# Two feed-forward layers in a one-core kernel: the first pair's down product as seven block products

## The chip, the cores and the metric

One core of a Trainium2 chip. The metric is the time of one execution in microseconds (us) of device time; below it is the median of 3 runs. In the profile PE is TensorE, DVE is VectorE, ACT is ScalarE, POOL is GpSimd, SP is SyncE, which issues most transfers.

## What is computed

One layer of a recurrent network on 1032 tokens (1024 of a prompt and 8 samples), width D = 1024, in float32. It begins and ends with a feed-forward layer of inner width 2816; between them lies a mixing stage, which the change leaves alone.

```python
def swiglu(x, w_gate, w_up, w_down):
    return (jax.nn.silu(x @ w_gate) * (x @ w_up)) @ w_down
...
    x = x + 0.5 * swiglu(rmsnorm(x, n1), f1g, f1u, f1d)
...
    x = x + m @ w_out
    x = x + 0.5 * swiglu(rmsnorm(x, n3), f2g, f2u, f2d)
```

## The kernel before

**Products.** A float32 operand is split into a high part (rounded, made by ACT) and a low part (the rest, made by DVE), and every product is three matmuls (`three`, L151): high x high, low x high, high x low. The halves of the input are 516 tokens each, and a matmul takes 258 tokens (columns) of one.

**Stages.** `ffn_tensor` (L585), `ffn_scalar`, `ffn_vector`, `ffn_gpsimd` and `ffn_sync` are the five engines' sides of one feed-forward layer. The layer is run twice, as `f1` and as `f2`. The inner width is 22 tiles, taken as 11 pairs. For the first pair, gate and up are eight plain products (`first_pair`, `plain`), each of 48 matmuls; the inputs are the four blocks B11, B21, B12, B22 (two row halves, two token halves). Every later pair i is a *group*: gate and up are seven products each (`product7`), by Strassen's scheme with the blocks B11, B21, B22 and four differences T1 to T4 of input blocks, and likewise seven weights (four of them sums of weight blocks, `unit_sums`). Each `product7` is 24 matmuls and leaves its result in a pair of PSUM banks; ACT copies some out (`snap`) and DVE adds others to them (`mix`), so that a later product may start on a pair only when the snap or mix of the one before is done.

**Down.** Group i (2 to 10) runs the down product of pair i-1 between its gate and its up (`down_pairs`): 7 blocks of hidden values, of which four are differences made by `hid_tees` on DVE, each split by ACT (`hid_high`) and DVE (`hid_low`); 168 matmuls. The parts that come out are added in DRAM to a running sum `x_sum` by accumulating transfers on POOL's queue (`ffn_gpsimd`). The down of the first pair is different: `down(True)`, a plain product of 24 output tiles of 344 tokens, 144 matmuls, right behind the first pair; DVE adds each tile to x (`add`), and then the updated x is copied to `x_sum` (8 transfers, L1260). Group 1 therefore has no down. The last pair's down is plain too, and is added to the x that has come back from `x_sum`.

**What sets the order.** Everything is written out by hand. Each engine works through its own list in order, and waits on counters of the others. Around the change these lists matter: on PE `first_pair`, `down(True)`, `group(1)`, then a loop over the groups; on ACT and DVE `first_pair`, `group_one` (and on DVE `behind_first` before it), then the loop. The T blocks of the input are made by DVE (`head_tees`), their high parts by ACT (`head_high`, L520), their low parts by DVE (`head_low`, L528); in the kernel before, T3, T1 and T4 are finished while PE runs `down(True)`. Weight slabs arrive in two buffers `raw` (`ffn_sync`). In the profile a weight's high part is L796 (L758 in the first pair), its low part L802 (L764), a weight sum L823, a snap L923, a mix L1082, a hidden product of the first pair L1045, an addition of `down` L1122, a hidden block's parts L858 and L865. DVE also does the model's small parameter arithmetic in group 1 of `f1` (`vector_between`, L3012 to L3028).

Of the kernel before, what the change touches and what calls it, by code (L numbers as in the profile page):

```python
# [32 lines left out]
NT = 3  # L33
# [25 lines left out]
FIRST_UNITS = 12  # L59
FIRST_SLABS = 6  # L60
FIRST_PRODUCTS = 8
LAST_DOWN = 3
DOWN_PAIRS = ((3, 2), (1, 0))
ADDED = 32 * (PAIRS - 1)
# [233 lines left out]
def units(i, n):  # L298

    return FIRST_UNITS + n if is_one(i) else i * 21 + (n + FIRST_UNITS + 14 - 42)  # L300


def prods(i, n):

    return FIRST_PRODUCTS + n if is_one(i) else i * 42 + (n + FIRST_PRODUCTS + 14 - 84)


def summed(i, n):

# [24 lines left out]

def prod_number(i, up, j):
    return (0, 7 if is_one(i) else 35)[up] + j + 1


def snap_number(i, up, n):
    return (0, 3 if is_one(i) else 19)[up] + n + 1  # L340


def mix_number(i, up, n):
    return (0, 3 if is_one(i) else 15)[up] + n + 1
# [16 lines left out]
def hid_count(i, j):  # L361
    return i * 7 + (32 - 7 + HID_ORDER.index(j) + 1)


def hid_tee(i, n):
    return i * 4 + (16 - 4 + n)
# [218 lines left out]
def ffn_tensor(pe, k, s):  # L585
    def plain(n, unit, pair, js, ready=None, between=None, parts=range(2), beside=None):

        for e in parts:
            pe.wait_ge(s.unit_lo, unit + e + 1)
            for g in range(2):  # L590
                if e == 1 and g == 1 and between:
                    between(pe)
                for kappa in range(KAPPAS):
                    if g == 0 and ready:
                        pe.wait_ge(s.norm.block_lo, block_count(js[e], kappa))
                    last = three(pe, k.bank[2 * pair + g][:, 0:QW], ffn_weight(s, (unit + e) % 6, kappa),
# [31 lines left out]
    def product7(i, up, j):  # L628

        pair = ((0, 2, 0, 1, 0, 1, 0), (2, 0, 2, 1, 2, 1, 2))[up][j]  # L630
        pe.wait_ge(s.unit_lo, units(i, unit_number(i, 2 * up, j)))
        if j in (T2, T3, T1, T4) and not up and is_one(i):
            pe.wait_ge(s.norm.block_lo, block_count(j, KAPPAS - 1))
        if j == 0:
            if not up:
                if is_one(i):
                    pe.wait_ge(s.down_used, KT * NT - 2)
                else:
                    pe.wait_ge(s.hidden, i * 4 - 3)
            elif is_one(i):  # L640
                pe.wait_ge(s.mixed, mixes(i, 1))
            else:
                pe.wait_ge(s.mixed, mixes(i, down_mix(1, 2, 1)))
        if j == 1:
            if not up:
                pe.wait_ge(s.hidden, i * 4)
            elif is_one(i):
                pe.wait_ge(s.silu, i * 4 + 4)
            else:
                pe.wait_ge(s.snap, snaps(i, down_snap(1, 3, 1)))  # L650
        if j == 2:
            pe.wait_ge(s.snap, snaps(i, snap_number(i, up, 0)))
        if j == 3 and up:
            if is_one(i):
                pe.wait_ge(s.mixed, mixes(i, 3))
        if j == 4:
            pe.wait_ge(s.snap, snaps(i, snap_number(i, up, 1)))
        if j == 5:
            pe.wait_ge(s.snap, snaps(i, snap_number(i, up, 2)))
        if j == 6:  # L660
            pe.wait_ge(s.mixed, mixes(i, mix_number(i, up, 1)))
# [7 lines left out]
    def down_pairs(i):  # L669

        for c in range(2):
            for j in range(7):
                if c == 0:
                    pe.wait_ge(s.unit_lo, units(i, unit_number(i, 1, j)))
# [11 lines left out]
    def four_ahead(i):  # L686

        pe.wait_ge(s.hidden_lo, s.hid_base + 5)
        pe.wait_ge(s.down_used, NT * KT)
        pe.wait_ge(s.mixed, mixes(i, mix_number(i, 1, 0)))  # L690
# [2815 lines left out]
```

## Time and profile before

| what | before |
|---|---|
| time, median of 3 runs | 2431.41 us (2430.89 to 2431.72) |
| span of the profiled execution (first to last instruction) | 2428.6 us |
| PE busy | 2415.6 us (99%), 19220 matmuls |
| DVE, ACT, POOL busy | 1739.7 us (72%), 1300.1 us (54%), 171.2 us (7%) |
| HBM traffic | 269.6 MB, 111 GB/s over the span |

The profile is one execution; its own time apart from its span is not given, so the median stands beside it, 2.8 us above the span. In a timeline row the first number is when the work began, the second how long it lasted; several equal instructions in a row are one line with their count. Successive instructions of one engine overlap a little: matmuls of 258 columns last 0.28 us each and start 0.12 us apart. In brackets stands how long the engine had been idle before, and what ended that. Idle time of an engine that holds nothing up costs nothing.

### The profile page before, as it was taken

The page shows a single profiled execution, that of the slowest core. Times are in us where ns is not written, and L with a number is a line of the kernel's source. Part 1 is how long each engine was busy: PE and PEld are TensorE (multiplying, and loading weights), DVE is VectorE, ACT ScalarE, POOL GpSimd, SP SyncE. Part 2 cuts the span into 40 slices and gives each one's busy share as a digit, 9 for nine tenths or more (in the row PEclk, how much of TensorE's full clock was granted, in tenths as well). Part 3 has the DMA queues.
Part 4 walks back from the last instruction along what each step waited for, and adds up shares of the span by engine and source line. Part 5 has one row for each costly group of instructions (what it writes and reads, how often), then busy time and mean ns, then how long its engine had stood idle before and what let it go on. Part 6 is the DMA issues. An engine that isn't in the chain of part 4 may idle for free.

```text
span 2428.6 us, 51528 instructions
## 1 busy us (share of the span) xinstructions
PE 2415.6 (99%) x19220; PEld 2400.9 (99%) x19220; DVE 1739.7 (72%) x2921; ACT 1300.1 (54%) x2206; POOL 171.2 (7%) x204
## 2 busy tenths in 40 slices
PE   9999999999999999999999999999999999999998
PEld 8999999999999999999999999999999999999998
DVE  8767767677689888887777775442676777777777
ACT  5355555555558676676666664211434555555554
POOL 0011111111120000000000000000200111111110
PEclk9999999999999999999999999999999999999999
DMA  4355555555541343333322235332023555555556
GB/s 144 106 123 121 121 121 121 122 121 121 135 182 54 95 114 81 88 97 100 109 90 87 69 138 178 140 131 87 18 103 88 123 122 122 122 122 122 122 123 197
DMA packets 137270, 278.34 MB, mean 115 GB/s; under 512 B 67024, under 2 KB 71632, under 8 KB 136656
## 3 DMA queue, kind: packets, MB, share of 16 engines
q1 hardware_dynamic: 114128, 192.39, 24.3%
q0 software_dynamic: 23040, 84.55, 18.4%
q8 instruction: 69, 1.13, 0.2%
q14 instruction: 33, 0.27, 0.0%
HBM read 154.80 MB, written 114.77 MB: 111 GB/s over the span
## 4 chain that ended last, share of the span: by engine, by line
PE 96%; DVE 2%; ACT 1%; DMA 1%; issue 0%; SPq 0%; DVEq 0%; ACTq 0%
PE banks L154 31%; PE banks L155 31%; PE banks L156 31%; PE banks L1819 1%; PE banks L1840 1%; PE banks L1850 1%; PE banks L1848 0%; PE banks L1854 0%; DMA x_sum<-f_snap 0%; DVE y L247 0%; DVE f_blk_f L504 0%; DMA raw<-w_slabs 0%; DVE f_blk_lo L528 0%; DVE x L1122 0%; ACT f_blk_hi L520 0%
## 5 line engine op out<-in xcount | busy, mean ns | idle before, releaser
L154 PE MATMUL banks<-f_blk_hi,f_u_hi 128*128 128x258 f32 x2496 | 706.7, 283 | 0.6 <-DVE f_blk_lo L528 0.4
L155 PE MATMUL banks<-f_blk_lo,f_u_hi 128*128 128x258 f32 x2496 | 705.6, 283 | 0.0
L156 PE MATMUL banks<-f_blk_hi,f_u_lo 128*128 128x258 f32 x2496 | 704.8, 282 | 0.0
L154 PE MATMUL banks<-mix_blk_hi,mix_u_hi 128*128 128x258 f32 x1808 | 515.0, 285 | 0.4 <-ACT mix_snap L1466 0.3
L155 PE MATMUL banks<-mix_blk_lo,mix_u_hi 128*128 128x258 f32 x1808 | 511.0, 283 | 0.0
L156 PE MATMUL banks<-mix_blk_hi,mix_u_lo 128*128 128x258 f32 x1808 | 510.2, 282 | 0.0
L154 PEld LDWEIGHTS banks<-f_blk_hi,f_u_hi 128*128 128x128 f32 x2496 | 471.4, 189 | 2.2 <-issue 1.1
L156 PEld LDWEIGHTS banks<-f_blk_hi,f_u_lo 128*128 128x128 f32 x2496 | 471.1, 189 | 0.0
L155 PEld LDWEIGHTS banks<-f_blk_lo,f_u_hi 128*128 128x128 f32 x2496 | 470.9, 189 | 0.2
L154 PEld LDWEIGHTS banks<-mix_blk_hi,mix_u_hi 128*128 128x128 f32 x1808 | 342.1, 189 | 1.0 <-issue 0.8
L155 PEld LDWEIGHTS banks<-mix_blk_lo,mix_u_hi 128*128 128x128 f32 x1808 | 341.6, 189 | 0.1
L156 PEld LDWEIGHTS banks<-mix_blk_hi,mix_u_lo 128*128 128x128 f32 x1808 | 341.4, 189 | 0.0
L154 PE MATMUL banks<-f_hb,f_u_hi 128*128 128x258 f32 x1008 | 285.3, 283 | 0.0
L155 PE MATMUL banks<-f_hb,f_u_hi 128*128 128x258 f32 x1008 | 284.9, 283 | 0.0
L156 PE MATMUL banks<-f_hb,f_u_lo 128*128 128x258 f32 x1008 | 284.5, 282 | 0.0
L1090 DVE TENSOR_TENSOR f_part<-banks,f_part 128x516 f32<-128x516 f32 x180 | 125.1, 695 | 152.7 <-PE banks L156 150.2
L931 ACT ACTIVATE f_part<-banks 128x516 f32<-128x516 f32 x252 | 151.7, 603 | 98.0 <-PE banks L156 79.3
L155 PEld LDWEIGHTS banks<-f_hb,f_u_hi 128*128 128x128 f32 x1008 | 191.1, 190 | 0.0
L156 PEld LDWEIGHTS banks<-f_hb,f_u_lo 128*128 128x128 f32 x1008 | 190.5, 189 | 0.0
L154 PEld LDWEIGHTS banks<-f_hb,f_u_hi 128*128 128x128 f32 x1008 | 190.3, 189 | 0.0
L796 ACT ACTIVATE f_u_hi<-f_sum 128x512 fp32r<-128x512 f32 x232 | 140.4, 625 | 84.5 <-PE banks L156 48.1
L802 DVE TENSOR_TENSOR f_u_lo<-f_sum,f_u_hi 128x512 fp32r<-128x512 f32 x232 | 156.1, 687 | 40.2 <-ACT f_u_hi L796 39.8
(306 smaller groups left out, 4378.3 us busy)
## 6 DMA issues: line engine op xcount, KB each, us to landing
raw<-w_slabs SPq DMA_DIRECT2D x220, 512.0 KB, 3.5
x_sum<-f_part POOLq DMA_DIRECT2D x126, 516.0 KB, 7.7
x_sum<-f_snap POOLq DMA_DIRECT2D x18, 516.0 KB, 10.2
x_sum<-x POOLq DMA_DIRECT2D x16, 516.0 KB, 5.8
x<-x_sum SPq DMA_DIRECT2D x16, 516.0 KB, 8.4
sg_kept<-sgt SPq DMA_DIRECT2D x8, 1032.0 KB, 5.7
sgs<-sg_kept SPq DMA_DIRECT2D x16, 516.0 KB, 4.5
x_kept<-x SPq DMA_DIRECT2D x1, 4128.0 KB, 12.1
```

The costliest lines, as they stand in the source:

```text
L154: pe.matmul(out, wh, xh, start=start, stop=False, skip_group_check=chained)
L155: pe.matmul(out, wh, xl, start=False, stop=False, skip_group_check=chained)
L156: return pe.matmul(out, wl, xh, start=False, stop=stop, skip_group_check=chained)
L796: act.activation(s.u_hi[j][:, :], unit_source(k, s, n, j), ACT.Copy).then_inc(s.unit_hi, 1)
L802: dve.tensor_tensor(s.u_lo[j][:, :], unit_source(k, s, n, j), s.u_hi[j][:, :].bitcast(F32), ALU.subtract)\
L931: act.activation(halves(part(s, c, kind)[:, q, :]), both(k, pair), ACT.Copy).then_inc(s.snap, 1)
L1090: dve.tensor_tensor(to, both(k, pair), to, ALU.add).then_inc(s.mixed, 1)
L1819: last = pe.matmul(k.bank[5][:, 0:P], s.ke[:, tok], s.qe[:, tok], start=True, stop=True)
L1840: pe.matmul(k.bank[6][:, at], s.kt[:, n, :], s.v[:, n, :], start=True, stop=True).then_inc(s.u_ready, 1)
L1850: last = pe.matmul(o[:, 0:P], s.v[:, n, :], s.sc[n % 2][:, :], start=n == 0, stop=True, skip_group_check=True)
```

## The change

The first pair's down moves into group 1 and takes the form that the other groups' downs have. So `down(True)`, the additions behind it, `group_one` and all special counts for group 1 go, and group 1 is an ordinary group. The hidden values of the first pair are written at once as hidden blocks, with the factor 0.5. The running sum begins with a copy of x as it was before the layer: in `f1` straight from the input in DRAM, from the first product on; in `f2` from x in SBUF once the stage before has written it, and since the hidden blocks of `f2` lie where x lies, the first hidden product waits for that copy. Of weights, the first pair has 8 units (12 before), and the slabs are stored in the new order.

```diff
-FIRST_UNITS = 12
-FIRST_SLABS = 6
+FIRST_UNITS = 8
+FIRST_SLABS = 4
@@ product7 (PE)
         if j == 0:
-            if not up:
-                if is_one(i):
-                    pe.wait_ge(s.down_used, KT * NT - 2)
...
+            if up:
+                pe.wait_ge(s.mixed, mixes(i, down_mix(1, 2, 1)))
             elif is_one(i):
-                pe.wait_ge(s.mixed, mixes(i, 1))
+                pe.wait_ge(s.silu, 4)
             else:
-                pe.wait_ge(s.mixed, mixes(i, down_mix(1, 2, 1)))
+                pe.wait_ge(s.hidden, i * 4 - 3)
@@ PE
     def group(i):
         for j in range(7):
             product7(i, 0, j)
-        if not is_one(i):
-            down_pairs(i)
+        down_pairs(i)
...
     first_pair()
-    down(True)
     group(1)
@@ weights
+def first_slot(u):
+
+    return u if u < 6 else u - 4
...
     if u >= 6:
-        act.wait_ge(s.prod, 4 + (u - 6) // 2)
+        act.wait_ge(s.prod, 5)
...
-    if is_one(i):
-        if n:
-            act.wait_ge(s.prod, prods(i, j + 1))
-        elif 2 <= j < 6:
-            act.wait_ge(s.down_ready, NT * KT)
-        else:
-            act.wait_ge(s.prod, FIRST_PRODUCTS)
+    if is_one(i) and n == 0:
+        act.wait_ge(s.prod, (4, 4, 8, 8, 6, 6, 8)[j])
@@ unit_sums (DVE)
+    if is_one(i) and n == 0:
+        dve.wait_ge(s.prod, FIRST_PRODUCTS)
@@ first_pair (ACT)
-        hidden_high(act, k, s, 0, 0)
+        for kappa in range(2):
+            head_high(act, k, s, T2, kappa)
+        silu_first(2)
         for u in (6, 7):
             first_high(act, k, s, u)
-        silu_first(2)
-        for u in (8, 9):
-            first_high(act, k, s, u)
+        for kappa in range(2, KAPPAS):
+            head_high(act, k, s, T2, kappa)
         silu_first(3)
-        hidden_high(act, k, s, 0, 1)
-        for u in (10, 11):
-            first_high(act, k, s, u)
-        for n, j in enumerate((T2, T3, T1, T4)):
+        for j in range(2):
+            unit_high(act, k, s, 1, 0, j)
+        for j in (T3, T1):
             for kappa in range(KAPPAS):
                 head_high(act, k, s, j, kappa)
-            if n < 2:
-                hidden_high(act, k, s, 0, 2 + n)
+        for j in range(2, 4):
+            unit_high(act, k, s, 1, 0, j)
+        for kappa in range(KAPPAS):
+            head_high(act, k, s, T4, kappa)
+        hid_high(act, k, s, 0, B11)
+        for j in range(4, 6):
+            unit_high(act, k, s, 1, 0, j)
+        hid_high(act, k, s, 0, B22)
+        hid_high(act, k, s, 0, B21)
@@ hidden_first (DVE)
-        gt = halves(s.gt[:, f, half(h)])
-        dve.tensor_tensor(gt, gt, both(k, (2, 1, 2, 3)[n]), ALU.mult).then_inc(s.hidden, 1)
+        if n == 0 and s.copied_out:
+            for kind in range(4):
+                dve.wait_ge(k.x_added[kind], s.added_base + 32)
+        dve.scalar_tensor_tensor(halves(hid_f(s, (B11, B12, B21, B22)[n])), halves(s.gt[:, f, half(h)]), 0.5,
+                                 both(k, (2, 1, 2, 3)[n]), ALU.mult, ALU.mult).then_inc(s.hidden, 1)
@@ group (DVE)
+        if is_one(i):
+            s.vector_between(dve)
         behind_up(i, last)
@@ ffn_gpsimd (POOL)
-    pool.wait_ge(s.down_used, NT * KT)
+    s.x_final(pool)
...
-    for i in range(2, PAIRS):
+    for i in range(1, PAIRS):
         group(i)
@@ build
+        f1.x_from, f2.x_from = x_t, k.x
+        f1.copied_out, f2.copied_out = False, True
+        f1.x_final = lambda pool: pool.wait_ge(f1.prod, 1)
+        f2.x_final = lambda pool: pool.wait_ge(o.unit_used, OUT_UNITS)
```

How ACT's list changes at the start of group 1's gate (blk_hi3, 4 and 5 are the high parts of T3, T1 and T4; u_hi0 to 6 the weights of the seven products; hb the hidden blocks; snap_122<-banks0 the first snap). Before:

```order
L520 ACTIVATE f1_blk_hi5_92<-f1_blk_f5_105 128x516 x4
L796 ACTIVATE f1_u_hi0_108<-raw0_69 128x512
L796 ACTIVATE f1_u_hi1_110<-raw0_69 128x512
L796 ACTIVATE f1_u_hi2_112<-f1_sum2_85 128x512
L796 ACTIVATE f1_u_hi3_114<-f1_sum1_84 128x512
L796 ACTIVATE f1_u_hi4_116<-f1_sum0_83 128x512
L796 ACTIVATE f1_u_hi5_118<-raw1_70 128x512
L923 ACTIVATE f1_snap_122<-banks0 128x516
L796 ACTIVATE f1_u_hi6_120<-f1_sum3_86 128x512
```

After:

```order
L775 ACTIVATE f1_u_hi2_112<-f1_sum2_85 128x512
L775 ACTIVATE f1_u_hi3_114<-f1_sum1_84 128x512
L518 ACTIVATE f1_blk_hi5_92<-f1_blk_f5_105 128x516 x4
L838 ACTIVATE f1_hb_126<-f1_hb_f_127 128x516
L775 ACTIVATE f1_u_hi4_116<-f1_sum0_83 128x512
L775 ACTIVATE f1_u_hi5_118<-raw1_70 128x512
L838 ACTIVATE f1_hb_126<-f1_hb_f_127 128x516 x2
L775 ACTIVATE f1_u_hi6_120<-f1_sum3_86 128x512
L910 ACTIVATE f1_snap_122<-banks0 128x516
L838 ACTIVATE f1_hb_126<-f1_hb_f_127 128x516 x4
L775 ACTIVATE f1_u_hi0_108<-raw0_69 128x512
L925 ACTIVATE f1_gt_82<-f1_gt_82 128x516
```

T4's parts, three hidden blocks and weight 6 now stand between the first weight sum that is used and the first snap, and four hidden blocks follow the snap. Behind the last row come one weight and the second snap.

DVE's list at the same place (blk_lo_102 and 104 are the low parts of T1 and T4, L804 the weight sums, L1011 the fourth hidden product, L856 to L861 the differences of hidden blocks, L1056 the first mix), after the change only; before, the additions L1122 stood between these, and no hidden block:

```order
L804 TENSOR_TENSOR f_sum_86<-raw_69,f_sum_85 128x512
L1011 SCALAR_TENSOR_TENSOR f_hb_f<-f_gt,banks 128x516
L781 TENSOR_TENSOR f_u_lo_113<-f_sum_85,f_u_hi_112 128x512
L781 TENSOR_TENSOR f_u_lo_115<-f_sum_84,f_u_hi_114 128x512
L526 TENSOR_TENSOR f_blk_lo_102<-f_blk_f_103,f_blk_hi_91 128x516 x4
L526 TENSOR_TENSOR f_blk_lo_104<-f_blk_f_105,f_blk_hi_92 128x516 x4
L781 TENSOR_TENSOR f_u_lo_117<-f_sum_83,f_u_hi_116 128x512
L781 TENSOR_TENSOR f_u_lo_119<-raw_70,f_u_hi_118 128x512
L845 TENSOR_TENSOR f_hb<-f_hb_f,f_hb 128x516 x3
L856 TENSOR_TENSOR f_hb_f<-f_hb_f 128x516
L857 TENSOR_TENSOR f_hb_f<-f_hb_f 128x516
L859 TENSOR_TENSOR f_hb_f<-f_hb_f 128x516
```

Behind these come the last difference (L861), weight 6, two splits of hidden blocks and the first mix. What moved: the splits of T1 and T4, spread over the plain down before, now stand in one piece ahead of the first hidden differences.

## Rows read from the trace of the kernel before

**Rows 1.** The page: busy time by engine, and the chain by engine.
```profile
PE 2415.6 (99%) x19220; PEld 2400.9 (99%) x19220; DVE 1739.7 (72%) x2921; ACT 1300.1 (54%) x2206; POOL 171.2 (7%) x204
...
PE 96%; DVE 2%; ACT 1%; DMA 1%; issue 0%; SPq 0%; DVEq 0%; ACTq 0%
```
**Rows 2.** Waits of PE over the span: us in total, times, longest.
```profile
PE banks L472 <- POOL reset L3395: 2.0, 1, 2.0
PE banks L464 <- DVE n_squares L436: 0.5, 1, 0.5
...
PE banks L154 <- ACT f_snap L923: 0.2, 1, 0.2
```
**Rows 3.** Timeline of PE: first matmul of the plain down and of group 1.
```profile
65.45 0.32 PE L154 MATMUL banks<-f_hid_hi,f_u_hi 128*128 128x344 f32 x1
...
88.44 0.28 PE L154 MATMUL banks<-f_blk_hi,f_u_hi 128*128 128x258 f32 x1
```
**Rows 4.** Timeline of POOL's queue: accumulations of groups 2 and 3; copies of `f2`.
```profile
153.99 0.93 POOL L1271 DMA_DIRECT2D x_sum<-f_part  x1 [51.54 <-DVE f_part L1090]
...
214.29 0.85 POOL L1271 DMA_DIRECT2D x_sum<-f_part  x1 [40.12 <-DVE f_part L1090]
...
1807.59 2.20 POOL L1260 DMA_DIRECT2D x_sum<-x  x3 [72.11 <-DVE x L1122]
...
1820.93 0.69 POOL L1260 DMA_DIRECT2D x_sum<-x  x1 [1.02 <-issue]
```
**Rows 5.** Timeline of DVE.
```profile
60.62 2.51 DVE L528 TENSOR_TENSOR f_blk_lo<-f_blk_f,f_blk_hi 128x516 fp32r<-128x516 f32 x4
...
65.65 0.69 DVE L1045 TENSOR_TENSOR f_gt<-f_gt,banks 128x516 f32<-128x516 f32 x1 [1.92 <-PE banks L156]
...
99.57 0.68 DVE L823 TENSOR_TENSOR f_sum<-raw 128x512 f32<-128x512 f32 x1
...
100.77 0.69 DVE L823 TENSOR_TENSOR f_sum<-f_sum,raw 128x512 f32<-128x512 f32 x1
...
102.22 0.69 DVE L802 TENSOR_TENSOR f_u_lo<-f_sum,f_u_hi 128x512 fp32r<-128x512 f32 x1
...
111.18 0.16 DVE L3012 TENSOR_TENSOR tmp<-tmp 128x8 f32<-128x8 f32 x1
...
115.18 0.69 DVE L802 TENSOR_TENSOR f_u_lo<-raw,f_u_hi 128x512 fp32r<-128x512 f32 x1
...
1736.56 0.51 DVE L2935 TENSOR_TENSOR x<-x,banks 128x344 f32<-128x344 f32 x1 [2.12 <-PE banks L156]
...
1754.99 0.69 DVE L1045 TENSOR_TENSOR f_gt<-f_gt,banks 128x516 f32<-128x516 f32 x1 [0.58 <-PE banks L156]
...
1847.85 0.69 DVE L876 TENSOR_TENSOR f_hb_f<-f_hb_f 128x516 f32<-128x516 f32 x1
...
1849.18 0.70 DVE L879 TENSOR_TENSOR f_hb_f<-f_hb_f 128x516 f32<-128x516 f32 x1
...
1850.53 0.68 DVE L802 TENSOR_TENSOR f_u_lo<-f_sum,f_u_hi 128x512 fp32r<-128x512 f32 x1
```
**Rows 6.** Timeline of ACT.
```profile
66.92 4.29 ACT L520 ACTIVATE f_blk_hi<-f_blk_f 128x516 fp32r<-128x516 f32 x8
...
1766.48 1.15 ACT L758 ACTIVATE f_u_hi<-raw 128x512 fp32r<-128x512 f32 x2 [4.10 <-PE banks L156]
...
1849.93 0.60 ACT L923 ACTIVATE f_snap<-banks 128x516 f32<-128x516 f32 x1 [2.17 <-PE banks L156]
```
**Rows 7.** The eighth copy of `f2` (1820.93): issue to landing, us.
```profile
DMA to landing us min/median/max: 5.7/5.7/5.7
```
**Rows 8.** Start: timeline of PE. Tail: stretches, with engine times, granted clock, transfers.
```profile
1.98 3.59 PE L472 MATMUL banks<-reset 128*128 128x512 bf16 x8 [1.98 <-POOL reset L3395]
...
10.91 1.89 PE L472 MATMUL banks<-reset 128*128 128x512 bf16 x8
...
2419.50:2422.70 3.20, 0.00 (x0) 0.00 (x0) 3.20 (x8) 1.02 (x2) 0.00 (x0) 1.00 0.94 334
2422.80:2428.60 5.80, 0.00 (x0) 0.00 (x0) 1.83 (x4) 0.00 (x0) 0.00 (x0) 0.50 0.85 295
```

More of the change, by code:

```diff
@@ L730, in ffn_tensor @@
     group(PAIRS - 1)
[L731 removed]
+    last_down()
 def slab_here(eng, k, s, i, c):
[L736 to L739 removed]
+    eng.wait_ge(k.slab_loaded[c % 2], i * 48 + 16 * (s.first // 2 + c // 2))
 def columns(b):
@@ L854, in hid_high @@
     if j in HID_IN:
-        act.wait_ge(s.hidden, i * 4 + {B11: 1, B22: 2, B21: 3}[j])
+        if is_one(i + 1):
+            act.wait_ge(s.hidden, {B11: 1, B21: 3, B22: 4}[j])
+        else:
+            act.wait_ge(s.hidden, i * 4 + {B11: 1, B22: 2, B21: 3}[j])
     else:
@@ L1029, in ffn_scalar @@
     first_pair()
-    for j in range(2):
-        unit_high(act, k, s, 1, 0, j)
-    group_one()
+    group(1)
     with act.Fori(2, PAIRS - 1) as i:
@@ L1057, in first_pair @@
         hidden_first(0)
-        hidden_low(dve, k, s, 0, 0)
-        for kappa in range(KAPPAS):
+        for kappa in range(2):
             head_tees(dve, k, s, kappa)
-            if kappa == 2:
-                hidden_first(1)
-                hidden_low(dve, k, s, 0, 1)
-            if kappa < 3:
-                for u in (6 + 2 * kappa, 7 + 2 * kappa):
-                    first_low(dve, k, s, u)
+        for u in (6, 7):
+            first_low(dve, k, s, u)
+        for kappa in range(2, KAPPAS):
+            head_tees(dve, k, s, kappa)
+        hidden_first(1)
+        low(T2)
+        for j in range(2):
+            unit_low(dve, k, s, 1, 0, j)
         hidden_first(2)
-        low(T2)
-        hidden_low(dve, k, s, 0, 2)
+        low(T3)
+        unit_sums(dve, k, s, 1, 0, (0, 1, 2, 3))
         hidden_first(3)
-        low(T3, range(2))
-        hidden_low(dve, k, s, 0, 3)
+        unit_low(dve, k, s, 1, 0, 2)
+        unit_low(dve, k, s, 1, 0, 3)
+        low(T1)
+        low(T4)
+        for j in range(4, 6):
+            unit_low(dve, k, s, 1, 0, j)
+        for j in (B11, B22, B21):
+            hid_low(dve, k, s, 0, j)
     def mix(i, up, n):
@@ L1110, in hidden, with add @@
             gt, to = halves(gt), halves(to)
-        if is_one(i) and n == 0:
-            for kind in range(4):
-                dve.wait_ge(k.x_added[kind], s.added_base + 32)
         dve.scalar_tensor_tensor(to, gt, 0.5, other, ALU.mult, ALU.mult).then_inc(s.hidden, 1)
-    def add(first, t, m):
+    def add(t, m):
         n = 8 * t + m
-        dve.wait_ge(s.down_ready, (0 if first else NT * KT) + n + 1)
-        if not first and m == 0 and t < 2:
+        dve.wait_ge(s.down_ready, n + 1)
+        if m == 0 and t < 2:
             dve.wait_ge(k.x_back[t], s.back_base[t] + 64)
@@ L1294, in ffn_sync @@
         load(s.first + c, c % 2)
[L1296 to L1307 removed]
+    def row(i, n, c):
+        if i == 1 and n == 0:
+            sp.wait_ge(s.unit_lo, (6, 8)[c])
+        else:
+            sp.wait_ge(s.unit_lo, units(i, 7 * (n - 1) + (2, 6)[c]))
+        if c == 0 and (i > 1 or n):
             sp.wait_ge(s.sums, summed(i, 4 * n))
         load(i * 6 + (s.first - 2 + 2 * n + c), c)
[L1311 removed]
+    for i in range(1, PAIRS):
         for n in range(3):
@@ L3444, in columns_apart @@
             return [rows[:, :, :, e].transpose(1, 0, 2, 3).reshape(P, D) for e in range(2)]
-        order = [*gate[:2], *up[:2], *down[:2], *gate[2:4], *up[2:4]]
-        for i in range(2, PAIRS):
+        order = [*gate[:2], *up[:2]]
+        for i in range(1, PAIRS):
             order += [*gate[2 * i:2 * i + 2], *columns_apart(i - 1), *up[2 * i:2 * i + 2]]
```

235 lines of the change are left out of this document (75 added, 160 removed).

## The prediction

> **What bounds the kernel now.** Read the busy shares and the chain first: TensorE (PE) is busy for 2415.6 of 2428.6 us and makes 96% of the chain that ended last [rows 1]. Then read who made PE wait: six entries over the whole span, 3.7 us together, 2.0 of them at the very start, and the others at most 0.5 each [rows 2]. So PE issues without a gap through both feed-forward stages, and the time can change in two ways only: fewer or shorter matmuls, or a wait that makes PE stand still. VectorE (72%) and ScalarE (54%) have spare time on average, but an average says nothing of one stage; there the order of their instructions decides.
>
> **What PE gains.** The plain down goes: 24 output tiles x 2 weights x 3 = 144 matmuls of 344 columns. They were issued from 65.45 to 88.44 [rows 3]: 22.99 us, 0.1597 each. In their place group 1 runs the down as blocks: 2 halves x 7 blocks x 2 x 2 x 3 = 168 matmuls of 258 columns. One whole loop group has 14 x 24 + 168 = 504 of these, and groups 2 and 3 are 60.30 us apart by the first accumulation that each sends (153.99 and 214.29) [rows 4]: 0.1196 each, with every hand-over inside. So 168 cost 20.09 us and PE gains **2.90 us in each of the two feed-forward layers, 5.8 us together**. It is less than the ratio 7/8 suggests. The rows have durations for both shapes, so they are used. The Trainium skill ("TensorE: Matmul & The Clock Gate", "Back-to-back issue gap") gives columns over 2.4 GHz plus 2.5 ns for one matmul behind another, 145.8 and 110.0 ns; by that estimate the exchange is worth 2.5 us per layer and the sum comes out 0.8 us worse. Both shapes are slower here than the page has them, the wide one by 14 ns, the narrow one by 10.
>
> **What stood behind the plain down.** In those 23 us ScalarE and VectorE finished splitting the blocks T3, T1, T4 and prepared group 1's first weights, and PE did not look at their results before 88.44. Now the first product of group 1 follows the eighth plain product at once. The eighth ends at 65.65, where VectorE's fourth hidden product had waited 1.92 us for it [rows 5]. I follow the two queues from there, in the new order.
>
> *First wait.* The product of T2 writes the banks that product B11 filled, so it waits for ScalarE's first snap. VectorE may make the weight sums only after the eighth product (the new wait in unit_sums). Four sums take 2.65 us, and the third, which weight 2 needs, is there 1.89 us after the first began (99.57, 100.77, 102.22) [rows 5]: 67.54. Behind that sum ScalarE has, by its new order, 12 instructions ahead of the snap: weights 2 and 3, four pieces of T4, hidden B11, weights 4 and 5, hidden B22 and B21, weight 6. Eight of this kind take 4.29 us, so one 0.525 us; a snap takes 0.60 [rows 6]. 67.54 + 6.30 + 0.60 = 74.44. PE has two products to do meanwhile, 48 x 0.1196 = 5.74 us from 65.45, until 71.19. **Wait: 3.25 us.** Before, the snap was ScalarE's fifth instruction there and nothing waited for it.
>
> *Second wait.* The product of T1 waits for the second snap, and ahead of that ScalarE must split hidden T2, T3, T1, T4, which need VectorE's hidden differences. VectorE's queue from 65.65: the sums 2.65, one hidden product 0.61, then 2 weights, 8 block pieces, 2 weights and 3 hidden blocks, 15 x 0.607 = 9.10 (four took 2.51, one 0.69, so 0.607 apart) [rows 5]; 78.01. The third difference starts 1.33 us after the first and takes 0.70, the four occupy 2.68 (1847.85, 1849.18, 1850.53) [rows 5]: T2 is there at 80.04, VectorE is free at 80.69. ScalarE: four splits and a weight, 5 x 0.525, until 82.67. Its next, silu 0, needs VectorE's mix, which stands behind a weight and two splits: 80.69 + 1.82 + 0.70 = 83.21. Then silu, a weight and the snap, 0.525 + 0.525 + 0.60: 84.86. PE: from 74.44 two products, until 80.18. **Wait: 4.68 us.** If ScalarE alone counted it would be 4.1 us; the mix sets the end. After it, the third snap comes 2.5 us behind the second and a product takes 2.87, so T4 is not held; mix 1 is due about 90.0 and B22 starts at 90.6, a margin of some 0.5 us.
>
> **Sum.** 3.25 + 4.68 - 2.90 = +5.03 us per layer. The second layer has the same queues and nearly the same distances, so the same sum: **+10.1 us**. Against the profiled execution's own span 2428.6 that is 2438.7. The median of the runs shown, 2431.41, lies 2.8 us over the span; what lies around the span is not changed. 2431.4 + 10.1 = **2441.5 us**, +0.4%.
>
> **Edits at nothing.** The 24 additions of the down and the splits of the hidden values for it go; the 16 differences of the input blocks only move to before the eighth product, where VectorE still waits for PE. The 12 part additions and 7 more weights of group 1 are what groups 2 to 10 do already with no PE wait [rows 2]; they lie beside 20 us of PE. So do the eight more accumulations on the POOL queue per layer; ScalarE waits for some in other groups and PE does not. If that cover went, PE would wait for a snap. The parameter arithmetic (111.18 to 115.18, 4.0 us) [rows 5] moves behind the block down of group 1; VectorE's waits for weights and banks around there take up most of it, and I keep 0 to 1 us of it for the range. The weight slabs come in another order but are as many after the first pair's; the copy of x in the first layer now starts near the first product, beside the slab loads, and has until about 90 us.
>
> **The copy of x in the second layer** can start once the last residual is written (1736.56 + 0.51) and VectorE's first hidden product now waits for it. Before, the first of eight was issued at 1807.59 and the last at 1820.93 [rows 4], which landed 5.7 us later [rows 7]: 19.0 us. So it lands at about 1756.1, 1.1 us after the 1754.99 at which that product ran [rows 5]. Behind it are 6.0 us of work (the product and eight differences), then a weight that ScalarE cannot make before the fifth product at 1766.48 [rows 6]. That leaves over 4 us of slack, so nothing.
>
> **Rivals.**
> *The clock falls in a wait.* The granted clock was 1.00 from start to last matmul. In the tail it stayed at 1.00 in 3.2 us with no PE work and stood at 0.50, the 1.2 GHz level, right behind [rows 8]. My second wait is longer than that, the first about as long. At the kernel's start eight matmuls of 512 columns took 3.59 us, later 1.89 [rows 8]: a fall costs at least 1.7 us, and up to twice that if the low level lasts longer. One fall in each layer at about 2 us: **2445.5 us**; four would be near 2449. For it: 4.7 is over 3.3. Against it: one event at the end tells little of where a fall comes. The Trainium skill ("TensorE: Matmul & The Clock Gate", "Why this matters for your kernels") warns of just such idle gaps between bursts of matmuls, since one brings the lower clock back. By that rule the time is this rival's; the tail agrees, and nothing else in this trace shows it.
> *It is covered, as in groups 2 to 10: not slower.* There the same ScalarE order (snap, four splits, weight, silu, weight, snap) holds no PE [rows 2]. The second snap comes 6.85 us after VectorE begins the hidden differences, and PE wants it at 71.19 + 5.74 = 76.93. If VectorE began them by 70.1 instead of 78.0, and the first snap were there by 71.2, both waits would vanish and the gain stand alone: **2425.6 us**. Against it: between the sums and that point stand a product and 15 instructions, of which two would fit.
> *The copy is late.* Landing later than about 1761 us delays VectorE, and once a second idle stretch is used up (the seventh product ends 5.74 us before the eighth, and 3.0 us of work follow it: 2.7 us) PE waits one for one. A copy of 29 us instead of 19.0 lands at 1766.1 and costs some 2 us: **2443.5 us**.
> *Another wait in group 1* (mix 1 with its margin of 0.5 us, or the parameter arithmetic): 1 to 2 us each, **2444 us**.
> *The change doesn't do what it says*, PE's matmuls staying as they are with the waits added: 2447 us; the rewritten order shows 168 in group 1, so this is hardly possible.
>
> **How the numbers follow.** Forecast 52%, clock 32%, covered 5%, late copy 3%, another wait 7%, last 1%. Bounds: each wait could be 1 us shorter if hand-overs run closer than in other stages, which over four waits gives 2437.5; the clock cases reach 2449. The range 2437.0 to 2448.5 leaves out the covered case, four falls and odds. A measurement of this kernel can tell 0.2%, 4.9 us, from no change. Only the covered case is faster. Within 0.2% needs the four waits to be 5.2 us shorter together than the 15.9 counted. So faster 0.05, same 0.07, slower 0.88.
>
> **What would show it.** In the new profile: PE waits of about 3.3 us at 71 and 4.7 us at 80 for ScalarE's snap, and the same two in the second layer some 1718 us later; PE's matmuls of 344 columns fewer by 288 and those of 258 more by 336; ScalarE's first snap of group 1 near 74; the granted clock 1.00 across both waits. Wrong would be: no such waits, waits at the hidden product of the second layer, a clock of 0.50 behind a wait, or a wait inside group 1's block down.

## The result, and the profile after

The changed kernel takes **2445.9 us** (median of 4 runs, 2445.03 to 2446.7); the kernel before, run beside it, 2431.15 us (4 runs, 2430.79 to 2431.72). The ratio is 1.0063, 95% interval 1.0051 to 1.0075: 14.75 us slower, where 10.1 were forecast. The profiled execution of the changed kernel took 2446.7 us, the longest of the four, and has a span of 2444.6 us. In five of the eight experiments too the profiled execution lies 0.7 to 2.9 us above its kernel's median, so sums of positions are held against spans and not against medians.

The page of the changed kernel (span, busy shares, chain), which answers to [rows 1]:

```profile
span 2444.6 us, 51756 instructions
PE 2419.6 (99%) x19268; PEld 2403.6 (98%) x19268; DVE 1751.6 (72%) x2925; ACT 1324.5 (54%) x2250; POOL 186.1 (8%) x220
PE 94%; DVE 3%; ACT 1%; DMA 1%; issue 1%; POOL 0%; DVEq 0%; ACTq 0%; POOLq 0%
```

PE still has 99% and nearly the same chain, so this view does not show the loss. The view of PE's waits does, against [rows 2]:

```profile
PE banks L156 <- ACT f_snap L910: 12.6, 5, 3.3
```

PE now waits five times for a snap of ScalarE, 12.6 us together. The timeline of PE shows where (the bracket is the idle time and what ended it):

```profile
74.50 0.36 PE L156 MATMUL banks<-f_blk_hi,f_u_hi 128*128 128x258 f32 x1 [3.27 <-ACT f_snap L910]
84.84 0.36 PE L156 MATMUL banks<-f_blk_hi,f_u_hi 128*128 128x258 f32 x1 [2.83 <-ACT f_snap L910]
127.36 0.36 PE L156 MATMUL banks<-f_blk_hi,f_u_hi 128*128 128x258 f32 x1 [0.38 <-ACT f_snap L910]
1801.48 0.36 PE L156 MATMUL banks<-f_blk_hi,f_u_hi 128*128 128x258 f32 x1 [3.27 <-ACT f_snap L910]
1811.83 0.36 PE L156 MATMUL banks<-f_blk_hi,f_u_hi 128*128 128x258 f32 x1 [2.83 <-ACT f_snap L910]
```

Four of them are the two forecast waits, at products T2 and T1 of group 1, once in each layer. They end where the two queues end them. ScalarE and VectorE in the first layer, against [rows 5, 6]:

```profile
67.50 1.15 ACT L775 ACTIVATE f_u_hi<-f_sum 128x512 fp32r<-128x512 f32 x2 [5.58 <-DVE f_sum L804]
73.78 0.58 ACT L910 ACTIVATE f_snap<-banks 128x516 f32<-128x516 f32 x1
79.91 2.21 ACT L838 ACTIVATE f_hb<-f_hb_f 128x516 fp32r<-128x516 f32 x4 [5.55 <-DVE f_hb_f L859]
84.12 0.58 ACT L910 ACTIVATE f_snap<-banks 128x516 f32<-128x516 f32 x1
...
65.51 0.69 DVE L804 TENSOR_TENSOR f_sum<-raw 128x512 f32<-128x512 f32 x1 [2.62 <-PE banks L158]
77.84 0.70 DVE L856 TENSOR_TENSOR f_hb_f<-f_hb_f 128x516 f32<-128x516 f32 x1
82.34 0.69 DVE L1056 TENSOR_TENSOR f_gt<-banks,f_snap 128x516 f32<-128x516 f32 x1
```

The first snap is done at 74.36 (forecast 74.44), the second at 84.70 (84.86). But ScalarE stood still for 5.58 us before 67.50 and VectorE for 2.62 us before 65.51: the lists are late and have gaps at the same time.

What was not in the sum is the clock. The sums of the first layer by stretches (columns: stretch, its length, then for PE, PEld, DVE, ACT, POOL the busy time and count, the granted clock, DMA share, GB/s):

```profile
71.00:74.40 3.40, 0.23 (x3) 0.03 (x1) 3.40 (x7) 3.36 (x7) 0.00 (x0) 1.00 0.00 1
74.40:75.20 0.80, 0.70 (x6) 0.73 (x7) 0.80 (x2) 0.00 (x0) 0.00 (x0) 1.00 0.00 0
75.20:78.60 3.40, 3.40 (x21) 3.40 (x20) 3.37 (x7) 0.00 (x0) 0.00 (x0) 0.58 0.47 130
84.60:85.40 0.80, 0.56 (x5) 0.59 (x5) 0.80 (x3) 0.10 (x1) 0.00 (x0) 1.00 0.00 0
85.40:88.90 3.50, 3.50 (x21) 3.50 (x20) 3.46 (x7) 1.64 (x3) 0.00 (x0) 0.59 0.00 0
```

Three matmuls in a row from the third of these stretches, in the timeline of PE:

```profile
76.01 0.42 PE L158 MATMUL banks<-f_blk_hi,f_u_lo 128*128 128x258 f32 x1
76.23 0.42 PE L156 MATMUL banks<-f_blk_hi,f_u_hi 128*128 128x258 f32 x1
76.44 0.42 PE L157 MATMUL banks<-f_blk_lo,f_u_hi 128*128 128x258 f32 x1
```

Through each wait the clock stayed at 1.00, and 1.1 to 1.5 us after PE had started again it fell to 0.50, the 1.2 GHz level (0.58 and 0.59 are means of stretches whose first part still ran at 1.00). Some 16 matmuls then start 0.216 instead of 0.12 us apart: **1.5 us** behind each of the four waits.

### The profile page after: what moved, and what is told of

Its sections match the earlier page's. It is cut to its first block, busy times and chain, and to the rows that moved or that the text cites. A ratio compares the mean times of both kernels' runs of the same rounds, so it can differ in the third digit from the quotient of the medians.

```text
span 2444.6 us, 51756 instructions
## 1 busy us (share of the span) xinstructions
PE 2419.6 (99%) x19268; PEld 2403.6 (98%) x19268; DVE 1751.6 (72%) x2925; ACT 1324.5 (54%) x2250; POOL 186.1 (8%) x220
## 4 chain that ended last, share of the span: by engine, by line
PE 94%; DVE 3%; ACT 1%; DMA 1%; issue 1%; POOL 0%; DVEq 0%; ACTq 0%; POOLq 0%
PE banks L156 30%; PE banks L157 30%; PE banks L158 30%; DMA x_sum<-f_snap 1%; DVE f_blk_lo L526 1%; PE banks L1750 1%; PE banks L1771 1%; PE banks L1781 1%; PE banks L1779 0%; PE banks L1785 0%; DVE y L249 0%; DVE f_blk_f L502 0%; PE banks L462 0%; DVE f_hb L845 0%; DVE f_u_lo L781 0%
## 5 line engine op out<-in xcount | busy, mean ns | idle before, releaser
L156 PE MATMUL banks<-f_blk_hi,f_u_hi 128*128 128x258 f32 x2496 | 710.7, 285 | 13.1 <-ACT f_snap L910 12.6
L156 PE MATMUL banks<-f_hb,f_u_hi 128*128 128x258 f32 x1120 | 317.0, 283 | 0.0
L157 PE MATMUL banks<-f_hb,f_u_hi 128*128 128x258 f32 x1120 | 316.5, 283 | 0.0
L158 PE MATMUL banks<-f_hb,f_u_lo 128*128 128x258 f32 x1120 | 316.1, 282 | 0.0
L1064 DVE TENSOR_TENSOR f_part<-banks,f_part 128x516 f32<-128x516 f32 x200 | 139.0, 695 | 169.5 <-PE banks L158 166.8
L918 ACT ACTIVATE f_part<-banks 128x516 f32<-128x516 f32 x280 | 168.3, 602 | 112.0 <-PE banks L158 87.4
L157 PEld LDWEIGHTS banks<-f_hb,f_u_hi 128*128 128x128 f32 x1120 | 212.3, 190 | 0.0
L158 PEld LDWEIGHTS banks<-f_hb,f_u_lo 128*128 128x128 f32 x1120 | 211.7, 189 | 0.0
L156 PEld LDWEIGHTS banks<-f_hb,f_u_hi 128*128 128x128 f32 x1120 | 211.5, 189 | 0.0
L1208 POOL DMA_DIRECT2D x_sum<-f_part x140 | 121.4, 867 | 1101.4 <-DVE f_part L1064 1022.0
L781 DVE TENSOR_TENSOR f_u_lo<-f_sum,f_u_hi 128x512 fp32r<-128x512 f32 x240 | 161.2, 687 | 41.8 <-ACT f_u_hi L775 41.8
## 6 DMA issues: line engine op xcount, KB each, us to landing
x_sum<-f_snap POOLq DMA_DIRECT2D x20, 516.0 KB, 10.4
```

What stands on the lines that cost most here:

```text
L156: pe.matmul(out, wh, xh, start=start, stop=False, skip_group_check=chained)
L157: pe.matmul(out, wh, xl, start=False, stop=False, skip_group_check=chained)
L158: return pe.matmul(out, wl, xh, start=False, stop=stop, skip_group_check=chained)
L781: dve.tensor_tensor(s.u_lo[j][:, :], unit_source(k, s, n, j), s.u_hi[j][:, :].bitcast(F32), ALU.subtract)\
L918: act.activation(halves(part(s, c, kind)[:, q, :]), both(k, pair), ACT.Copy).then_inc(s.snap, 1)
L1064: dve.tensor_tensor(to, both(k, pair), to, ALU.add).then_inc(s.mixed, 1)
```

## The account of the 14.75 us

Products T2 and T3 together took 7.35 us instead of 5.74 because of the first fall. So PE came later to the second wait, and that wait shrank by as much, since its end is set elsewhere. From last matmul to first, less one normal step, PE stood 3.42 and 2.99 us; 3.42 + 1.61 + 2.99 = 8.0 us, where the forecast had 3.25 + 4.68 = 7.9. **The first fall costs nothing, the second costs its 1.5 us.** With the forecast's sum that gives 10.1 + 2 x 1.5, about 13.2 us.

The trace of the changed kernel also shows what PE gains. These are the first matmul of group 1's block down and the first behind it:

```profile
95.08 0.28 PE L156 MATMUL banks<-f_hb,f_u_hi 128*128 128x258 f32 x1
115.28 0.29 PE L156 MATMUL banks<-f_blk_hi,f_u_hi 128*128 128x258 f32 x1
```

The 168 matmuls took 20.20 us here and 20.14 in the second layer, against 22.99 [rows 3] and 22.98 for the plain down. The gain is 2.8 us a layer, 5.6 together, where the forecast had 5.8.

The rest is small and spread out. Rows of the timeline of POOL and of ScalarE, to hold against [rows 4] (POOL issues a transfer, ScalarE makes the second snap of up):

```profile
100.02 0.93 POOL L1208 DMA_DIRECT2D x_sum<-f_part  x1 [56.42 <-DVE f_part L1064]
116.96 0.85 POOL L1208 DMA_DIRECT2D x_sum<-f_snap  x1 [2.24 <-issue]
161.16 0.86 POOL L1208 DMA_DIRECT2D x_sum<-f_part  x1 [39.86 <-DVE f_part L1064]
403.74 0.87 POOL L1208 DMA_DIRECT2D x_sum<-f_part  x1 [40.22 <-DVE f_part L1064]
464.88 0.88 POOL L1208 DMA_DIRECT2D x_sum<-f_part  x1 [39.65 <-DVE f_part L1064]
...
126.62 0.60 ACT L910 ACTIVATE f_snap<-banks 128x516 f32<-128x516 f32 x1 [4.73 <-DMA x_sum<-f_snap]
430.38 0.60 ACT L910 ACTIVATE f_snap<-banks 128x516 f32<-128x516 f32 x1 [4.57 <-DMA x_sum<-f_snap]
```

Group 2 begins its accumulations 61.1 us behind group 1, and group 7 61.1 us behind group 6; undisturbed groups follow at 60.5 to 60.6. One part of the down lies in the two snap slots, so the second snap of up may be made only when the transfer out of them has landed. At 126.62 that came so late that PE waited 0.38 us for it, and at 430.38 PE's next matmul started 0.40 instead of 0.12 us behind the one before. From group 1 to group 10 this adds 2.0 us in the first layer and 0.6 in the second, taken against the kernel before's mean distances of 60.55 and 60.47. In the profiled execution 13.2 + 2.6 = 15.8, or 16.0 with the gain as measured, stands against a difference of spans of 16.0; the median of the runs is a little better. Not all of the 2.6 us can be put down to group 1's new accumulations: some 0.9 us lie between groups 1 and 3 of the first layer, the rest lies between groups 6 and 9, where both kernels send the same eight accumulations per group, and it is spread otherwise in every trace (filled has 1.1 us in all). Why the kernel before has almost none of it is not shown.

## Experiments

All times are medians beside runs of the kernel before on the same chip (2430.2 us for snap_early, snaps_early, filled and new_order, 2430.1 for the others), so differences to it are compared; the changed kernel's is +14.75.

| kernel | us | against before | ratio (95% interval) |
|---|---|---|---|
| snap_early | 2446.0 | +15.8 | 1.0064 (1.0048 to 1.0079) |
| snaps_early | 2444.4 | +14.2 | 1.0056 (1.0041 to 1.0072) |
| filled | 2440.8 | +10.6 | 1.0043 (1.0029 to 1.0057) |
| filled_in_part | 2441.4 | +11.3 | 1.0047 (1.0031 to 1.0062) |
| new_order | 2428.6 | -1.6 | 0.9991 (0.9982 to 1.0000) |
| rotated_after | 2443.5 | +13.3 | 1.0054 (1.0040 to 1.0067) |
| rotated_new_order | 2427.4 | -2.8 | 0.9986 (0.9977 to 0.9995) |
| rotated_before | 2429.8 | -0.3 | 0.9999 (0.9990 to 1.0009) |

### snap_early: remove the first wait alone

```diff
+        snap(1, 0, 0)
         for kappa in range(KAPPAS):
             head_high(act, k, s, T4, kappa)
...
         unit_high(act, k, s, i, 0, 6)
-        snap(i, 0, 0)
+        if not is_one(i):
+            snap(i, 0, 0)
```

> One edit on ScalarE in both layers: the first snap of group 1 stands right behind weights 2 and 3 instead of behind ten more instructions. Theory (the queues set the ends of the waits, TensorE only fills what lies before them): the wait of product T2 goes; the wait of product T1 still ends where ScalarE and VectorE end it, near 84.8 us, and grows from 2.8 to about 7.8 us. One fall of the clock per layer goes with the first wait, but it was hidden in the second wait. So two falls instead of four, and the time stays within 0.5 us of the changed kernel's 2445.9 us. Rival (each wait and each fall costs by itself): 3.3 + 1.5 us less per layer, 2436.4 us. Second rival (ScalarE's list is not what holds product T2): a wait of about 3.3 us at T2 stays.

The timeline of PE at product T1 in the first layer:

```profile
85.03 0.56 PE L156 MATMUL banks<-f_blk_hi,f_u_hi 128*128 128x258 f32 x1 [7.85 <-ACT f_snap L911]
```

And the sums of the stretch behind it:

```profile
85.00:88.30 3.30, 3.27 (x15) 3.30 (x16) 3.27 (x7) 1.64 (x3) 0.00 (x0) 0.50 0.00 0
```

The wait at product T2 is gone from the trace and nothing is gained. The second wait ends at 85.03 instead of 84.84 and is 7.85 us long. Here the clock fell inside the wait, and PE began behind it at 1.2 GHz at once, for 19 matmuls (27 in the second layer, 12 and 18 in snaps_early below), 1.2 to 2.6 us in place of the changed kernel's 1.5. The theory of the queues holds. The rival's 2436.4 us would be a ratio of 1.0022, below the interval. (+15.8 and +14.75 can't be told apart by these runs.)

### snaps_early: all three gate snaps early

```diff
+        if is_one(i):
+            snap(i, 0, 1)
+            snap(i, 0, 2)
         hid_high(act, k, s, i - 1, T2)
         hid_high(act, k, s, i - 1, T3)
```

(with the edit above, and with the two snaps left out further down.)

> ScalarE alone is reordered, in both layers: the first snap of group 1 right behind weights 2 and 3, the second and third ahead of the splits of the hidden differences. VectorE's list is unchanged. Theory (VectorE's list is the second bound): no wait at T2 and none at T1; TensorE stands at the seventh gate product instead, for mix 1, which VectorE reaches near 89.2 us; 89.9 against 82.7 is a wait of about 7.2 us, with one fall of the clock behind it. The seventh product then ends at about 94.3 instead of 95.0 us: 0.7 us less per layer, 2444.5 us. Rival (ScalarE's order alone is to blame): no long wait is left and the gain of the exchange stands, 2426 to 2428 us.

PE's waits, and its timeline in the first layer:

```profile
PE banks L156 <- DVE f_gt L1063: 14.3, 2, 7.2
```

```profile
89.83 0.55 PE L156 MATMUL banks<-f_blk_hi,f_u_hi 128*128 128x258 f32 x1 [7.14 <-DVE f_gt L1063]
```

The place is as the theory has it, to 0.1 us: 89.83 for 89.9, a wait of 7.14 for 7.2. (The time, +14.2 against +14.75, is no measurable gain.) The wait moved from ScalarE's snap to VectorE's mix. So ScalarE's order alone was not the cause: three limits lie one behind the other, and taking the first two away uncovers the third.

### filled and filled_in_part: keep PE busy in the waits

```diff
+        if is_one(i) and not up and j in (2, 4):
+            pe.wait_ge(s.hidden, 4)
+            for n in range(8 if j == 2 else 12):
+                three(pe, k.bank[6][:, 0:QW], ffn_weight(s, j, n % KAPPAS), ffn_rows(s, j, n % KAPPAS, 0),
+                      True, True, chained=True)
         if j == 2:
             pe.wait_ge(s.snap, snaps(i, snap_number(up, 0)))
```

(3 and 6 in place of 8 and 12 in the second kernel.)

> The waits stay, but TensorE does not stand idle in them: 24 matmuls of 258 columns whose result nobody reads go ahead of product T2 in group 1 and 36 ahead of product T1, in both layers (2.9 and 4.3 us of work against waits of 3.4 and 4.5 us). They write a bank that is free then. Theory (idle time brings the clock down; the first fall of each layer is hidden in the second wait, the second is not): granted clock 1.00 through both layers, and 1.5 us less per layer: 2442.8 us. Rival (every fall costs 1.5 us): 2439.8 us. Second rival (the falls have another cause than idle time): four falls remain and the time is 2445.9 us or a little more.

> As the filled kernel, with fewer matmuls in the waits: 9 and 18 instead of 24 and 36, so that TensorE stands still for about 2.3 us in each of the four waits. In the changed kernel it stood for 3.3 and 2.8 us, each time with a fall behind. Theory (a stand of 2.3 us is too short to bring the clock down): 1.00 throughout and the time of the filled kernel, 10.6 us over the kernel before. Rival (any stand of over 2 us does it): two to four falls, 13 to 14 us over.

Of filled, two stretches of 60 us around group 1 of either layer (its only waits for a snap are two of 0.3 us):

```profile
60.00:120.00 60.00, 59.71 (x495) 59.35 (x494) 47.53 (x90) 33.17 (x60) 6.94 (x8) 1.00 0.45 103
1785.00:1845.00 60.00, 59.68 (x496) 59.29 (x495) 45.27 (x74) 32.60 (x58) 6.98 (x8) 1.00 0.48 108
```

The clock is 1.00 throughout with the snaps as late as ever (the first is done at 74.45 instead of 74.36). Here idle time is what brings it down. On the size, the time does not decide: it came out at 2440.8 us, between the theory's 2442.8 and the rival's 2439.8, and both lie in the interval. The positions in the traces decide: group 1's first accumulation is issued at 98.55 us instead of 100.02, 1.5 us earlier with two falls gone. So one of the two had cost nothing. The kernel stands 10.6 us over the one before, which is the forecast's own sum of 10.1 and some tenths. Of its 4.1 us under the changed kernel 3 are the two falls; in the profiled executions the rest is shorter distances between the groups (1.1 instead of 2.6 us too long).

Of filled_in_part, the two waits of the first layer in PE's timeline:

```profile
74.19 0.39 PE L156 MATMUL banks<-f_blk_hi,f_u_hi 128*128 128x258 f32 x1 [2.10 <-ACT f_snap L915]
84.53 0.39 PE L156 MATMUL banks<-f_blk_hi,f_u_hi 128*128 128x258 f32 x1 [0.61 <-ACT f_snap L915]
```

And the stretches behind them:

```profile
74.20:79.90 5.70, 5.70 (x34) 5.70 (x35) 5.60 (x10) 0.22 (x1) 0.00 (x0) 0.70 0.29 92
84.50:90.00 5.50, 5.47 (x45) 5.47 (x46) 5.02 (x9) 2.06 (x4) 0.00 (x0) 1.00 0.23 36
```

My theory was wrong here: in both layers a fall came behind a stand of 2.1 us. But it was hidden in the second wait, which it cut from the intended 2.3 to 0.61 us, and behind that one there was none. Hence one fall in each layer and still the time of filled; group 1's first accumulation is issued at 98.22 us, 98.55 in filled. The first fall of the pair is free, shown a second time. A third showing stands under rotated_after.

### new_order: both lists rewritten

Group 1's lists on ScalarE and VectorE were written anew, from the last gate silu of the first pair to the first half of the block down, with the same instructions. Their order (T a quarter of an input block, w a gate weight, v a down weight, h a hidden block, S a gate snap, m a gate mix, g a silu, s, t and r the sums for gate, down and up, x3 the last hidden product, tees the hidden differences, p a part of the down):

```diff
+ACT_ORDER = """
+T3 T3 T3 T3 T1 T1 T1 T1 T4 T4 T4 T4 w2 w3 hB11 hB22 hB21 S0 w4 w5 w6 v0 S1 S2 v1 g0 hT2 hT3 hT1 g1
+hT4 g2 g3 v2 v3 v4 p00 p01 v5 p10 p11 p20 v6 p21 p30 p31
+DVE_ORDER = """
+T3 T3 T3 T3 T1 T1 T1 s0 s1 s2 x3 s3 T1 w2 T4 w3 T4 w4 T4 w5 T4 hB11 w6 hB22 v0 hB21 m0 tees m1 hT2
+t0 hT3 hT1 t1 m2 hT4 t2 v1 t3 v2 v3 v4 p00 p01 v5 p10 v6 p11 p20 p21 r0 r1 r2 r3
```

> Both lists of group 1 are rewritten, in both layers, with the same instructions: ScalarE splits T4 and the first hidden blocks in the 5.6 us in which it stood waiting for the weight sums and makes each snap as soon as its product is there; VectorE splits T1 in its 2.6 us of waiting before the sums, and makes the mixes of the gate ahead of the splits of the hidden differences, and the parts of the down ahead of the sums for up. Theory (only the order of the two lists made the waits): no wait of TensorE over 1 us, no fall of the clock, and the exchange gives its 5.8 us less 1 to 3 us of small waits: 2426.5 to 2428.5 us, under the kernel before. Rival (the work for the block down does not fit beside seven products, whatever the order): waits of 2 us and more inside group 1's block down, and 2431 us or more.

Its waits of PE, beside those of the start that every kernel has:

```profile
PE banks L156 <- ACT f_part L944: 1.0, 3, 0.6
PE banks L156 <- ACT f_snap L936: 0.8, 1, 0.8
```

All four long waits are gone, no fall is left, and some 16 us with them. The work for the block down does fit beside seven products. What remains are waits of up to 0.8 us, at the accumulations again. From group 1 to group 10 this kernel needs 2.2 us more in each layer than the distances of the kernel before would give, and that takes most of the 5.6 us. So it falls short of what was expected: 1.6 us under the kernel before, where 5.8 less 1 to 3 us were to be left. Its interval just reaches 1.0000, so these runs hardly tell it from the kernel before. Which of the many moves did it was not tried one by one.

### rotated_after, rotated_new_order, rotated_before: who uses the snap slots

```diff
-    return s.snap_t[:, 1:3, :] if c == 1 and kind == 2 else s.part[kind][:, :, :]
+    if c == 1 and kind == 0:
+        return s.snap_t[:, 1:3, :]
+    return s.part[0 if c == 1 and kind == 2 else kind][:, :, :]
```

(with the waits of `down_part` and of the snaps of up turned to the transfers that now matter.)

> The changed kernel with the buffers of the down parts in another rotation, in every group of both layers: the part that lies in the two snap slots is now the first of the second half (its transfer is issued some 7 us earlier), and the third part of the second half takes the buffer of the first part of the first half. Theory (what the sum left over is the second snap of up, which ScalarE may make only when the transfer out of its slot has landed): groups 1 to 10 follow each other at 60.5 to 60.6 us everywhere, 2.4 us less in all, so 12.3 instead of 14.7 us over the kernel before. Rival (the longer periods have another cause, such as memory traffic or a new wait on the other buffer): periods of 61 us remain and the time is 14 to 15 us over.

> The new order of both lists of group 1 together with the rotated buffers. Theory: the wait of 1.0 us in group 1's up and the longer periods after it (0.7 us in the first layer, 0.8 in the second) go too; 2 us less than the new order alone, 3.5 to 4 us under the kernel before on the same chip. Rival (the buffer that is now written twice in a group holds ScalarE inside the block down): no gain on the new order, 1.6 us under the kernel before or less.

> The kernel before with the rotated buffers alone. Theory (there the groups already follow each other at 60.5 to 60.6 us, so nothing is left to gain): no difference, within 0.5 us. Rival (the rotation is worth something by itself): 1 to 2 us less.

Of rotated_after, the accumulations of groups 6 and 7, and the second snap of up in group 1:

```profile
403.68 0.87 POOL L1212 DMA_DIRECT2D x_sum<-f_part  x1 [39.96 <-DVE f_part L1066]
464.26 0.88 POOL L1212 DMA_DIRECT2D x_sum<-f_part  x1 [40.43 <-DVE f_part L1066]
...
124.85 0.60 ACT L910 ACTIVATE f_snap<-banks 128x516 f32<-128x516 f32 x1 [2.25 <-DVE f_snap L1058]
```

The snap no longer waits for a transfer, and the mean distance of the groups is 60.58 and 60.47 us, what it is in the kernel before; one of 60.84 is left. That takes 2.3 us out of the distances and 1.8 out of the span. The difference in time, +13.3 after +14.75, points the same way, but it lies between theory (12.3) and rival (14 to 15) and the two intervals overlap. In the kernel before the rotation is worth nothing, as expected.

This trace shows one thing more. The two waits of the first layer, and the stretch behind the first of them:

```profile
74.39 0.36 PE L156 MATMUL banks<-f_blk_hi,f_u_hi 128*128 128x258 f32 x1 [3.27 <-ACT f_snap L910]
84.73 0.55 PE L156 MATMUL banks<-f_blk_hi,f_u_hi 128*128 128x258 f32 x1 [4.33 <-ACT f_snap L910]
75.20:78.60 3.40, 3.40 (x31) 3.40 (x30) 3.37 (x7) 0.00 (x0) 0.00 (x0) 1.00 0.48 147
```

The first wait is as long as in the changed kernel, 3.27 us, but behind it the clock stayed at 1.00. PE came to the second wait 1.5 us earlier, and that wait was 1.5 us longer: 4.33 instead of 2.83. It ended at 84.73, in the changed kernel at 84.84. So the first fall costs nothing, here with no edit to the products or the gate's snaps. And the length of a stand alone did not decide whether the clock fell.

Of rotated_new_order, the two long waits in PE's timeline:

```profile
110.66 0.36 PE L156 MATMUL banks<-f_blk_hi,f_u_hi 128*128 128x258 f32 x1 [1.95 <-ACT f_part L946]
1829.40 0.36 PE L156 MATMUL banks<-f_blk_hi,f_u_hi 128*128 128x258 f32 x1 [1.89 <-ACT f_part L946]
```

And the stretches behind them:

```profile
110.60:114.80 4.20, 4.14 (x25) 4.17 (x26) 3.22 (x17) 1.45 (x3) 0.87 (x1) 0.69 1.06 273
1827.50:1835.00 7.50, 5.61 (x47) 5.63 (x47) 3.71 (x6) 3.25 (x6) 1.72 (x2) 1.00 1.07 247
```

Here theory and rival are both right in part: the snap is free, but in group 1 ScalarE waits for the transfer out of a part's buffer (4.4 us in the first layer) and holds PE for 1.9 us. That its transfers follow each other more quickly than in other groups is the likely reason, not tested. Two waits of 1.9 us remain in this trace, whose execution was the slowest of eleven (2430.3 us against a median of 2427.4), so the others may have less of them. By its median it is the fastest kernel of the study, **0.14% under the kernel before, interval 0.05 to 0.23%**, of the 5.8 us (0.24%) that the forecast had for the exchange of the matmuls. From new_order these runs can't tell it apart, since the intervals overlap.

## Why the prediction was right, and where it was short

- *The sign and the range were right*: slower, 2445.9 inside 2437.0 to 2448.5. The predicted time was 4.4 us low. The range's upper end comes from the clock rivals, and one of the prediction's own signs of being wrong, a clock of 0.50 behind a wait, came true. That the result lies 0.4 us from the clock rival's 2445.5 is in part luck: it had one fall a layer at 2 us, the traces have two, of which one costs 1.5 us, and the rest came from the distances between the groups.
- *The gain on PE* (2.90 us a layer) was right: 2.8 in both layers of the trace. It is borne out by filled, which has the waits but no fall, at +10.6 for a sum of 10.1. Only the remark that it is less than the ratio 7/8 suggests was wrong: 22.99 / 8 is 2.87.
- *Both waits* were right in place, cause and end: 74.36 and 84.70 for 74.44 and 84.86. (In the second layer they came 1727 us later and not 1718, since the first layer's own loss had been left out of that distance.) That the mix sets the second end, not ScalarE alone, is shown by snaps_early, where it alone does.
- *The step that failed is the sum's silence on the clock*, which counted falls at nothing. I had it as a rival at 32% and gave the forecast 52%, with the argument that one event at the kernel's end tells little. It fell behind each of the four waits. My price for it was then too high, about 2 us a fall and near 2449 for four: a fall costs 1.5 us in the changed kernel, and two of the four lie in the shadow of a later wait. Four falls cost 3 us, not 8. The rows that I took the price from [rows 8] show no fall of the granted clock either. The eight matmuls at the start took about twice the later time, but the sums of the kernel before give 1.00 for their stretch:

```profile
2.00:5.50 3.50, 3.50 (x9) 1.32 (x10) 0.69 (x1) 0.66 (x2) 0.00 (x0) 1.00 0.99 331
```

  The rule cited from the Trainium skill ("TensorE: Matmul & The Clock Gate", "Why this matters for your kernels") held in the changed kernel, in all four waits of 3.3 and 2.8 us, and it should have carried the likeliest case. It did not hold once, behind the 3.27 us in rotated_after.
- *"Eight more accumulations on POOL at nothing"* was the second step that failed: by 0.9 us next to group 1 in the profiled execution, and by at most some 1.5 us of the median with the delays in later groups, whose cause stays open. I had named the cover (PE would wait for a snap if it went), but not how much was left of it. It was about zero: ScalarE already waited 3.6 us on average for that transfer in the kernel before, up to 4.6, and a few tenths more reach PE.
- *The copy of x in the second layer* was right. VectorE waited for it and lost it again in a later idle stretch:

```profile
1764.69 0.69 DVE L1011 SCALAR_TENSOR_TENSOR f_hb_f<-f_gt,banks 128x516 f32<-128x516 f32 x1 [1.51 <-DMA x_sum<-x]
1775.90 1.29 DVE L748 TENSOR_TENSOR f_u_lo<-raw,f_u_hi 128x512 fp32r<-128x512 f32 x2 [5.18 <-ACT f_u_hi L742]
```

  It landed about 18.5 us after the first of its transfers was issued (19.0 in the forecast).
- *Parameter arithmetic and mix 1* made no wait of PE, so the 7% for another wait in group 1 went to neither; a wait of 0.38 us came from the accumulations instead.
- *The covered case* (5%) named what was missing, VectorE's earlier start on the differences, and said that of 15 instructions only two would fit. new_order shows that the estimate was of the old order only: with ScalarE's pieces of T4 and three of VectorE's of T1 in the idle time ahead of the sums, and the snaps and mixes early, both long waits go and the kernel is not slower. The case's 2425.6 us, 5.8 under, was not reached.

What stays open: whether the last two waits of 1.9 us can be ordered away as well; why the longer distances between later groups are rare in the kernel before; and what else than its length decides whether a stand brings the clock down.

## What to carry to other kernels

When waits follow each other and the end of the last one is set by other engines, price the last one's end only; what happens before it (an earlier wait, a slower clock) is absorbed as long as it is shorter than the last wait. In these traces 14 of 15 stands of 1.95 us and more in the layers brought the clock down, at a price of 1.2 to 2.6 us behind the wait. So add a fall to such a wait, but only where no further wait follows to hide it. And before a block of work that other engines prepared in the shadow of something is pulled forward, look for the stretches in which those engines stand idle just ahead: here lists that use part of such 5.6 and 2.6 us, with snaps and mixes made early, took away the loss of 14.75 us and came out 1.6 us under the kernel before, and 2.8 with the rotated buffers.

## What the runs showed of the hardware that was not expected

- Stands of TensorE and the clock in these runs: behind 3.27, 2.83, 2.1 (twice) and 1.95 us it fell, behind 1.89, 0.8 and 0.6 us it did not, and neither behind one of 3.27 us (rotated_after, first layer). In those of 4.3, 7.1 and 7.9 us, and in two of 3.27 and 2.96 us (rotated_after, second layer), it fell before the wait was over. Between 1.89 and 1.95 us lies no rule that these runs could show. Behind the waits 12 to 27 matmuls of 258 columns ran at the 1.2 GHz level, 0.096 us each too slow.
- An accumulating transfer of 516 KB out of the snap slots took 10.4 us from issue to landing (median, changed kernel), one from the part buffers 7.8, a plain copy of x of the same size 6.3. The Trainium skill ("DMA: Bandwidth & Descriptors", "Anatomy of one DMA — SWDGE (gpsimd) path") has 2.0 us plus the bytes at 436 KB per us, an estimate of 3.2 us for this size. With several under way at once, as here, the fastest plain copy of x in the changed kernel came near it at 3.4 us; the medians and every accumulating transfer (5.2 us at least) are longer.
